# Rows of a partition packed together in the down matrices of a mixture-of-experts kernel, and the gate and up columns read with a step of four

## What is computed

```
def hier_moe(x, norm_g, w_rg, w_re, w_gate, w_up, w_down):
    u = rms_norm(x, norm_g)
    ...                                  # group of 4, then the 2 best of its 4 experts: dense_w (rows, 16)
    h = jax.nn.silu(jnp.einsum('ntd,edf->ntef', u, w_gate)) * jnp.einsum('ntd,edf->ntef', u, w_up)
    h = h * dense_w[..., None].astype(h.dtype)
    return jnp.einsum('ntef,efd->ntd', h, w_down)
```

## Time and profile before

| | |
|---|---|
| time, median of 3 runs (lowest to highest) | 1483.19 us (1480.87 to 1484.49) |
| span of the profiled execution, which is all the time that the profile gives for it | 1482.9 us |
| mean granted TensorE clock, as a share of 2.4 GHz | 0.941 |
| TensorE busy / its weight loads busy | 91% / 69% |
| VectorE, ScalarE, GpSimd busy | 35%, 21%, 12% |
| DMA, mean over the span | 295 GB/s |

### The profile page before, as it was taken

One profiled execution on the slowest core, in us unless ns is written; L12 is line 12 of the kernel. 1 busy time (PEld: TensorE's weight loads), 2 busy tenths in 40 slices (PEclk: granted clock), 3 DMA queues, 4 the chain that ended last, 5 costly groups with the idle time before them and its releaser, 6 DMA issues.

```text
span 1482.9 us, 37368 instructions
## 1 busy us (share of the span) xinstructions
PE 1346.8 (91%) x15938; PEld 1027.1 (69%) x15938; DVE 518.5 (35%) x1163; ACT 309.1 (21%) x728; POOL 173.7 (12%) x206
## 2 busy tenths in 40 slices
PE   5998999999887889998989899989996799999996
PEld 5888888888535666766665556556445788888883
DVE  3351110000175546464646766663024200000005
ACT  2130100000142221313133443434011000010110
POOL 1012000000302000111111111210000300000002
PEclk9899999999988999999999998997997899999998
DMA  9269999999996679797978997974263589999985
GB/s 307 84 249 307 383 392 393 390 388 388 367 362 225 221 247 358 257 370 267 334 241 274 295 308 240 331 256 158 95 269 135 153 302 384 388 385 385 385 331 187
DMA packets 147690, 437.15 MB, mean 295 GB/s; under 512 B 21319, under 2 KB 51912, under 8 KB 138607
## 3 DMA queue, kind: packets, MB, share of 16 engines
q1 hardware_dynamic: 99319, 367.64, 67.7%
q10 hardware_dynamic: 37296, 38.09, 7.6%
q0 software_dynamic: 10960, 29.80, 6.7%
HBM read 406.38 MB, written 29.45 MB: 294 GB/s over the span
## 4 chain that ended last, share of the span: by engine, by line
PE 47%; DMA 24%; issue 13%; DVE 7%; ACT 4%; SPq 3%; ACTq 1%; POOL 1%; POOLq 0%; DVEq 0%
DMA W<-in_w_up 18%; PE PS L1276 9%; PE PS L1411 5%; PE PS L1039 4%; PE PS L1072 3%; PE PS L1067 3%; PE PS L1035 3%; PE PS L1317 2%; PE PS L976 2%; PE PS L1355 2%; PE PS L1375 2%; PE PS L1363 2%; PE PS L968 1%; DMA out_k_prompt<-W 1%; DMA W<-in_cache_v 1%
## 5 line engine op out<-in xcount | busy, mean ns | idle before, releaser
L1035 PE MATMUL PS<-W,KV 128*32 128x384 f32 x3072 | 343.4, 488 | 15.3 <-DMA W<-in_w_up 10.6
L1039 PE MATMUL PS<-W,KV 128*32 128x128 f32 x3072 | 346.4, 274 | 0.0
L1039 PEld LDWEIGHTS PS<-W,KV 128*32 128x32 f32 x3072 | 334.2, 110 | 1.4
L2119 DVE TENSOR_TENSOR KV<-KV,PS 128x384 f32<-128x384 f32 x32 | 17.7, 554 | 479.6 <-PE PS L1053 443.6
L1276 PE MATMUL PS<-W 128*128 128x256 f32 x768 | 181.1, 390 | 0.7 <-ACT KV L1681 0.7
L1276 PEld LDWEIGHTS PS<-W 128*128 128x128 f32 x768 | 146.5, 196 | 32.4 <-issue 10.4
L1067 PE MATMUL PS<-W,KV 128*32 128x384 f32 x1440 | 163.9, 493 | 3.5 <-ACT KV L1587 3.5
L1072 PE MATMUL PS<-W,KV 128*32 128x256 f32 x960 | 163.9, 329 | 0.0
L1035 PEld LDWEIGHTS PS<-W,KV 128*32 128x32 f32 x3072 | 141.0, 110 | 22.7 <-DMA W<-in_w_up 16.5
L2260 DVE STREAM_TRANSPOSE KV<-KV 128x1024 f32<-128x1024 f32 x128 | 154.8, 1225 | 0.0
L1072 PEld LDWEIGHTS PS<-W,KV 128*32 128x32 f32 x960 | 96.0, 110 | 15.1 <-issue 0.2
(11 more groups left out here) (293 smaller groups left out, 1581.0 us busy)
## 6 DMA issues: line engine op xcount, KB each, us to landing
W<-in_w_gate SPq DMA_DIRECT2D x32, 2048.0 KB
W<-in_w_up SPq DMA_DIRECT2D x32, 2048.0 KB, 22.0
W<-in_w_down SPq DMA_DIRECT2D x32, 2048.0 KB, 11.5
KV<-in_cache_k SPq DMA_DIRECT2D x256, 256.0 KB, 5.3
W<-in_cache_v SPq DMA_DIRECT2D x128, 512.0 KB, 7.9
yd<-KV ACTq DMA_DIRECT2D x30, 288.0 KB, 7.0
W<-in_w_kvf SPq DMA_DIRECT2D x4, 2048.0 KB, 25.8
W<-in_w_kvf ACTq DMA_DIRECT2D x8, 1024.0 KB, 8.3
```

The source lines that it names most:

```text
L1035: pe.matmul(PS[32 * q:32 * q + 32, bank, 0:WIDE], x, w[:, k, 0:WIDE], start=(k == 0), stop=(k == KC - 1), tile_position=(0, 32 * q), skip_ ...
L1039: mm = pe.matmul(PS[CAP:P, bank, P * q:P * q + P], x, w[:, k, WIDE:FF], start=(k == 0 and q == 0), stop=(k == KC - 1), tile_position=(0, C ...
```

## The change

It changes the order of the hidden features of an expert. A down matrix is loaded with four consecutive rows in each partition, in one run of 16 KB: partition p holds hidden features 4p to 4p + 3. So slice f of the hidden values must be the features f, f + 4, f + 8 and so on, and the gate and up products read their weight columns in that order: column n of slice f is column 4n + f of the matrix, a step of four float32 (16 bytes) between neighbours of the moving operand. The gate and up loads, the stationary operands, the numbers and shapes of all matmuls, the code of `down` and all semaphores stay.

```
         def w_src(l, e, which):
             if which < 2:
                 return A["w_gate" if which == 0 else "w_up"][l, e].rearrange("(p k) f -> p (k f)", k=KC)
-            return A["w_down"][l, e].rearrange("(f p) n -> p f n", f=FC)
+            return A["w_down"][l, e].rearrange("(p f) n -> p (f n)", f=FC)
...
-            return t[bass.ds(e, 1)].rearrange("e (f p) n -> p (e f) n", f=FC)
+            return t[bass.ds(e, 1)].rearrange("e (p f) n -> p (e f n)", f=FC)
 
         def w_slot(slot, which):
-            return W[:, slot, :] if which < 2 else W[:, slot, :].rearrange("p (f n) -> p f n", f=FC)
+            return W[:, slot, :]
+
+        def hidden_columns(slot):
+
+            return W[:, slot, :].rearrange("p (k n f) -> p k f n", k=KC, f=FC)
...
                 def product(bank, slot, count, name):
                     pe.wait_ge(sem(f"w_in_{slot}"), count + l * (8 * NE))
-                    w = W[:, slot, :].rearrange("p (k n) -> p k n", k=KC)
+                    w = hidden_columns(slot)
                     for k in range(KC):
                         for q in range(Q4):
                             x = XT[:, k, 32 * q:32 * q + 32]
-                            pe.matmul(PS[32 * q:32 * q + 32, bank, 0:WIDE], x, w[:, k, 0:WIDE], start=(k == 0),
+                            pe.matmul(PS[32 * q:32 * q + 32, bank, 0:WIDE], x, w[:, k, 0:FC - 1, :], start=(k == 0),
                                       stop=(k == KC - 1), tile_position=(0, 32 * q), skip_group_check=True)
                         for q in range(Q4):
                             x = XT[:, k, 32 * q:32 * q + 32]
-                            mm = pe.matmul(PS[CAP:P, bank, P * q:P * q + P], x, w[:, k, WIDE:FF], start=(k == 0 and q == 0),
+                            mm = pe.matmul(PS[CAP:P, bank, P * q:P * q + P], x, w[:, k, FC - 1, :], start=(k == 0 and q == 0),
                                            stop=(k == KC - 1), tile_position=(0, CAP), skip_group_check=True)
...
-                                w = W[:, which, :].rearrange("p (k n) -> p k n", k=KC)
+                                w = hidden_columns(which)
                                 for k in range(KC):
-                                    mm = pe.matmul(PS[:, 2 + which, :], XT[:, k, :], w[:, k, :], start=(k == 0), stop=(k == KC - 1))
+                                    mm = pe.matmul(PS[:, 2 + which, :], XT[:, k, :], w[:, k], start=(k == 0), stop=(k == KC - 1))
```

## The result

| | median of the runs | runs |
|---|---|---|
| before | 1483.84 us (1480.87 to 1488.72) | 4 |
| after | 1830.89 us (1827.73 to 1831.42) | 4 |

The changed kernel takes 1.2338 times as long (95% interval 1.2292 to 1.2384). The profiled execution has a span of 1829.6 us against 1482.9 us before, 346.7 us more. In the changed kernel all lines behind the edit have a number four higher: L1039 is the wide matmul of a product (L1035 before), L1043 the tail (L1039 before), L1071 and L1076 are `down`.

The account below looks back on a forecast made before the run. The expert blocks were taken as DMA-bound by little, TensorE close behind. Stepped columns add 327 us and remove 12 us of waits, the down load's gain vanishing: 1482.9 + 327 - 12 = 1798 us, range 1469 to 1825 us.

Parts of the forecast that it names:

- What bounds it, and how much cover there is: Expert blocks: DMA-bound by little, 18.0 to 18.2 us an expert against TensorE's 17.83; waits total 12.2 us.
- The mechanism: Gate and up products: stepped columns read at half the rate, TensorE needing 28.0 us an expert against 18 of DMA.
- All signs that were named: Expert blocks: slice 1.29 us for 0.65, chain through product matmuls, up waits near 0, DMA share near 0.65, `down` unmoved.
- the column term: Gate and up products: 12288 columns an expert at 0.832 ns more each, 10.2 us an expert, 327 us for 32.
- half the rate: Products' moving operand: a stepped column costs 0.83 ns more; chance 0.62 including prices between the bounds.
- The upper bound: Products' columns: at most 0.88 ns more each, from stationary loads with step 16; 346 us less 12, 1817 us.
- the argument against a smooth fall: Products' reads: steps 16, 8 and 4 all put elements 16 bytes or more apart, so shared reads serve one element each.
- The down load: Down matrices in 16 KB runs: 0.17 us less an expert, 4.8 us in all, gone if TensorE sets the pace.
- the step is free: Rival, gate and up products: stepped reads cost nothing, only the down load's gain stays, 1478 us; chance 0.27.
- four tiles share one read path: Rival, gate and up products: tiles take turns reading, a column costs four times as much, 2452 us; chance 0.09.

Follow-up runs that it names:

- e1: Kernel before with only the down matrices loaded in 16 KB runs, products still reading neighbours: 1506.27 us, ratio 1.0030 to the kernel before.
- e1_again: The kernel before with only the 16 KB down loads, products reading neighbours, run a second time: 1505.55 us, ratio 0.9991.
- e2: Kernel before with only the step of four in the gate and up products, down loads still in 4 KB runs: 1841.12 us, ratio 1.2240.
- e4 to e6: Kernel before with step four only in the middle stage's single-matmul projection (ratio 1.0970), only in the products' wide tiles (1.223), only in their tail tile (1.228).
- the pairs: Kernel before with the products' moving operand read as two neighbours out of every eight float32: 1492.12 us, ratio 1.007.
- the null: The kernel before, unchanged, run and profiled once more beside the experiments: 1481.03 us, ratio 0.9986.
- e10: Kernel before with 16 KB down loads and no stepped read; VectorE writes hidden values reordered, transposes cut into more, smaller matmuls: 1575.89 us, ratio 1.0461.

## Why the prediction was wrong

- **What bounds it, and how much cover there is: right.** The loads had 12.2 us of slack to give in all. TensorE has no wait for a weight matrix left in either block; in 103 to 570 us of the changed kernel it waited only for these (total us, times, longest):

```profile
PE PS L1071 <- ACT KV L1591: 2.7, 1, 2.7
PE PS L1039 <- DVE KV L1956: 1.6, 2, 1.1
```

- **The mechanism: right.** Every column of the products is read at about half the rate, the slice waits for it, and the DMA engines idle. All signs that were named came in kind: a slice of 1.36 us (1.29 was said), the chain, no waits, a DMA share of 0.61 (0.65 was said), `down` at its old durations.
- **The failing step is the size of the column term.** The prediction took 0.83 ns more for a column, "half the rate", between bounds of 0 and 0.88 ns from the stationary loads of the earlier trace rows. Measured is 1.758 - 0.832 = 0.926 ns more (spacing of the tail records: 229 against 109 ns over 128 columns, 0.94 ns). The upper bound was too low as well: an expert costs 11.4 us more and not 10.2 us, the kernel 12288 x 32 x 0.926 ns = 364 us and not 327 us. 1482.9 + 364 - 12 = 1835 us, 5 us above the measured span. The term that it put too low is the price of a column, not the number of columns or what waits for them. So 1798 us was 33 us too low, and the measured time lies 6 us above the range.
- **Why the bound was wrong.** Two readings of the rows went into it. "Half the rate" was a guess at a round factor, not a row; the price isn't tied to TensorE's own rate, since it is the same at the lower clock, where a column of neighbours costs twice as much (last section). And the fall from step 16 (0.88 ns) over step 8 (0.41 to 0.52 ns) in the earlier trace rows was read as a possible fall with the step. Step 8 costs the products 1.79 ns and step 4 1.758 ns: from one element a piece on, the step no longer matters, as the argument against a smooth fall had it. So what differs between those rows may be the kind of load; that was argued and not tried, and why a stationary load shows a lower price than a moving operand stays open.
- **The down load: cheaper for the DMA engines, unproven for the kernel, and worth nothing here.** Runs of 16 KB brought e1 and e1_again no gain in time that can be told from none, though the 0.17 us an expert of the prediction is not refuted (0.13 us in the windows above). In the changed kernel TensorE sets the pace, so they could not have helped: e2, without them, has the same expert (29.27 us).
- **The rival "the step is free"** fell by e2, with the step alone at 1.224. **The rival "four tiles share one read path"** fell by e4 to e6: one stream pays the same 1.76 ns as four, and a stepped stream does not slow one beside it.

The Trainium skill's rule (Advanced Engine Details and Errata, section SBUF Cachelines), lines of 16 bytes and at least two hits on a line for full performance, agrees with these runs in its kind: step 2 and the pairs have two hits and cost 0.887 and 0.898 ns, step 3 has 4/3 and costs 1.32 ns, steps 4 and 8 have one and cost 1.758 and 1.79 ns. The sentence on the skill's page SBUF — State Buffer (Door 1: The DMA port swizzle), that one can stride for free up to "4 fp32", does not hold as it stands: a step of 4 costs 2.1 times the column, and the last step that is nearly free is 2.

## What to carry to other kernels

When a layout change turns a TensorE operand from neighbours into a step, count new pieces of 16 bytes for each element and price the moving operand's columns by them (here the larger of 0.83 ns and 1.76 ns times the pieces, for float32 at full clock) before weighing any gain on the DMA side. The stream with the step must be the one that nobody waits for: here even one stepped tile of four cost everything, because the four end together. And a bound taken from another kind of instruction wants a margin: the stationary load's 0.88 ns was 5% below what the moving operand cost, and the range, up to 1825 us, had too little room for it.

## What the runs showed that was not expected

**The step costs next to nothing at the lower clock.** The two records of a product, wide and then tail, where the granted clock was 0.50 (1.2 GHz), in the kernel before (1160.1 to 1163.4 us), in the changed kernel (1335.4 to 1339.7 us) and with step 3 (1247.4 to 1251.4 us):

```profile
L1035 PE MATMUL PS<-W,KV x18: 574/844/846, 1160.1 to 1163.3; 128*32 128x384 f32 x18
L1039 PE MATMUL PS<-W,KV x16: 358/418/419, 1160.1 to 1163.3; 128*32 128x128 f32 x16
L1039 PE MATMUL PS<-W,KV x21: 853/860/877, 1335.4 to 1339.5; 128*32 128x384 f32 x21
L1043 PE MATMUL PS<-W,KV x19: 405/408/422, 1335.4 to 1339.6; 128*32 128x128 f32 x19
L1035 PE MATMUL PS<-W,KV x21: 717/837/846, 1247.4 to 1251.3; 128*32 128x384 f32 x21
L1039 PE MATMUL PS<-W,KV x19: 378/410/420, 1247.4 to 1251.3; 128*32 128x128 f32 x19
```

A column of neighbours takes 1.66 ns there, twice the 0.832 ns of full clock. With the step of four it takes 1.77 ns, as at full clock (1.758), and with step 3 1.67 ns, where full clock has 1.32. So of the two prices only that of the neighbours follows TensorE's clock; the 1.76 ns of a new piece does not, and "half the rate" is half of the rate at full clock. The DMA engines were nearly idle in all three stretches (share 0.02), so the price isn't contention with the loads either. These are few records, some 20 in a group.

**The first experts of two sets.** In the first and third set the first expert of each block took 25 to 31 us, whatever was edited (e1_again 26.2 and 27.0 us, step 2 26.1 and 26.5 us), against 12.9 and 14.5 us in the trace of before and in the null. That is about the 23 us by which the kernel before itself was slower there; it was not profiled in these sets. TensorE's waits of e1_again in 103.7 to 130 us (total us, times, longest):

```profile
PE PS L1039 <- issue: 3.9, 6, 1.7
PE PS L1035 <- DVE KV L1952: 1.6, 2, 1.1
PE PS L1035 <- issue: 1.4, 3, 0.6
```

The null has no such "issue" rows there. They are 5.3 us, under half of the 13.4 us: TensorE was also busy for 20.3 us with the same 205 records that took 12.4 us in the null, at a granted clock of 0.87 against 1.00. In layer 1 it is the same at a DMA share of 0.33, so full loads are not what it takes. The cause stays open. With a step of four the first expert takes 30.5 and 29.9 us (e2) against 24.6 and 24.5 us (the changed kernel), 11 us in all, which is about e2's excess of 10 us. So the two kernels of a set don't lose the same, the ratios of the stepped kernels in the first and third set are up to 1% too low, and gains of a few us in e1 can hide in it.

**The clock of e10.** The changed kernel, TensorE busy without a gap, keeps 1.00 (2.4 GHz) from the second to the fourteenth expert of both blocks, at 29.27 us each. In e10 TensorE was as busy, with full-rate reads and more small matmuls; in layer 0 the mean was 0.92 in the second to sixth expert, 1.00 in the next five and 0.92 in the three after them, so that some of each slower expert passed at the lower level (1.2 GHz). Why is open. The granted clock alone then costs 20.6 - 19.0 = 1.6 us an expert, more than the added transposes do.
